# 64 bytes between the rings of split weights and their neighbours, and one slot instead of six for two small vectors

## The reference

```python
mod = (c_act @ w_ada + b_ada).reshape(B, N_MOD, 1, D_MODEL)
x = x + 0.5 * mod[:, 2] * swiglu(modulate(rmsnorm(x, norm_w[0]), mod[:, 0], mod[:, 1]), ffn1_wi, ffn1_wo)
h = modulate(rmsnorm(x, norm_w[1]), mod[:, 3], mod[:, 4])
zq, zk, zv, zb, zc, zu, zga, zgb = jnp.split(h @ w_in, splits, axis=-1)
o_attn = windowed_attention_with_context(q, k, v, kc, vc, sink)
y_conv = zb * short_conv(zc * zu, conv_w)
x = x + mod[:, 5] * gated_merge(o_attn, y_conv, zga, zgb, w_oa, w_ob, w_out)
x = x + 0.5 * mod[:, 8] * swiglu(modulate(rmsnorm(x, norm_w[2]), mod[:, 6], mod[:, 7]), ffn2_wi, ffn2_wo)
```

## Time and profile before

| | |
|---|---|
| time, median of 2 runs | 1981.53 us (1979.94 and 1983.12) |
| span of the profiled execution | 1978.3 us |
| granted clock of TensorE, mean over the span | 0.998 of full speed |
| TensorE busy | 1944.9 us, 98% of the span |
| VectorE busy | 867.2 us, 44% |
| ScalarE busy | 695.4 us, 35% |
| DMA engines, mean rate | 137 GB/s |

### The profile page before, as it was taken

One profiled execution on the slowest core, in us unless ns is written; L12 is line 12 of the kernel. 1 busy time (PEld: TensorE's weight loads), 2 busy tenths in 40 slices (PEclk: granted clock), 3 DMA queues, 4 the chain that ended last, 5 costly groups with the idle time before them and its releaser, 6 DMA issues.

```text
span 1978.3 us, 27290 instructions
## 1 busy us (share of the span) xinstructions
PE 1944.9 (98%) x10403; PEld 1587.5 (80%) x10403; DVE 867.2 (44%) x1337; ACT 695.4 (35%) x1050; POOL 92.1 (5%) x153
## 2 busy tenths in 40 slices
PE   6999999999999999999999999999999999999998
PEld 4666688887888888666668888888888889999998
DVE  4422333236665355433333226333322487666554
ACT  2422233124434324322233115333321355545543
POOL 1011100000000001111110000000000000000000
PEclk9999999999999999999999999999999999999999
DMA  8667622232222223666753222332332244446552
GB/s 300 221 220 250 234 86 97 94 85 81 74 70 64 75 94 119 233 234 224 240 192 97 96 90 80 96 95 95 96 96 95 64 129 128 141 137 191 181 190 97
DMA packets 183071, 271.17 MB, mean 137 GB/s; under 512 B 25196, under 2 KB 146268, under 8 KB 183004
## 3 DMA queue, kind: packets, MB, share of 16 engines
q1 hardware_dynamic: 164572, 203.12, 32.6%
q0 software_dynamic: 18432, 67.12, 10.1%
HBM read 269.16 MB, written 1.05 MB: 137 GB/s over the span
## 4 chain that ended last, share of the span: by engine, by line
PE 94%; DVE 4%; DMA 1%; ACT 0%; issue 0%; POOL 0%; SPq 0%; DVEq 0%; ACTq 0%
PE ps L440 29%; PE ps L442 28%; PE ps L441 28%; PE ps L464 4%; DVE T L1086 1%; DVE hL L1093 1%; PE ps L540 1%; PE ps L681 1%; PE ps L554 1%; PE ps L499 1%; DVE wL L1016 1%; PE ps L476 1%; DMA xin<-in_ctx 0%; PE ps L493 0%; PE ps L495 0%
## 5 line engine op out<-in xcount | busy, mean ns | idle before, releaser
L1016 DVE TENSOR_TENSOR wL<-raw,wH 128x1024 fp32r<-128x1024 f32 x364 | 442.4, 1224 | 668.5 <-ACT wH L804 666.9
L440 PE MATMUL ps<-hH,wH 128*128 128x512 f32 (+1 forms) x1984 | 714.8, 360 | 1.2 <-DVE hL L1348 0.9
L442 PE MATMUL ps<-hH,wL 128*128 128x512 f32 (+1 forms) x1984 | 703.6, 355 | 0.0
L441 PE MATMUL ps<-hL,wH 128*128 128x512 f32 (+1 forms) x1984 | 702.2, 354 | 0.0
L804 ACT ACTIVATE wH<-raw 128x1024 fp32r<-128x1024 f32 x364 | 383.1, 1058 | 685.0 <-PE ps L442 680.4
L440 PEld LDWEIGHTS ps<-hH,wH 128*128 128x128 f32 x1984 | 374.9, 189 | 97.6 <-issue 45.7
L442 PEld LDWEIGHTS ps<-hH,wL 128*128 128x128 f32 x1984 | 374.9, 189 | 53.9
L441 PEld LDWEIGHTS ps<-hL,wH 128*128 128x128 f32 x1984 | 375.3, 189 | 50.0
L440 PE MATMUL ps<-GH,wH 128*128 (+2 forms) x704 | 256.6, 365 | 0.0
L441 PE MATMUL ps<-GL,wH 128*128 (+2 forms) x704 | 256.6, 365 | 0.0
L442 PE MATMUL ps<-GH,wL 128*128 (+2 forms) x704 | 256.6, 365 | 0.0
(11 more groups left out here) (138 smaller groups left out, 1393.3 us busy)
## 6 DMA issues: line engine op xcount, KB each, us to landing
raw<-in_ffn_wi SPq DMA_DIRECT2D x176, 512.0 KB, 3.6
raw<-in_ffn_wo SPq DMA_DIRECT2D x88, 512.0 KB, 3.5
adaA<-in_w_ada POOLq DMA_DIRECT2D x64, 512.0 KB, 4.7
adaB<-in_w_ada POOLq DMA_DIRECT2D x64, 512.0 KB, 4.7
raw<-in_w_in SPq DMA_DIRECT2D x60, 512.0 KB, 3.9
raw<-in_w_out SPq DMA_DIRECT2D x16, 512.0 KB, 3.6
ada0b<-in_w_ada SPq DMA_DIRECT2D x4, 1024.0 KB, 13.6
raw<-in_w_in SPq DMA_DIRECT2D x32, 128.0 KB, 2.7
```

The lines of the kernel that those rows point to most:

```text
L440: mm(dst, wa, ra, start=start, stop=False, **kw)
L441: mm(dst, wa, rb, start=False, stop=False, **kw)
L442: return mm(dst, wb, ra, start=False, stop=stop, **kw)
L1016: tt(wL[:, s, :], raw[:, s, :], wH[:, s, :].bitcast(F32), ALU.subtract).then_inc(lo_done, 1)
```

## The change

Two arrays of 16 floats (64 bytes a partition) that nothing reads or writes are placed ahead of `wH` and behind `wL`. `normA` and `gateH` shrink from six slots to one, that is by 320 bytes each, and each norm and each residual now overwrites the slot of the one before. No instruction is added or removed and no wait is changed.

```diff
         raw = sb("raw", [P, RING, PIECE])
+        sb("beside_wH", [P, 16])
         wH = sb("wH", [P, RING, PIECE], F32R)
         wL = sb("wL", [P, RING, PIECE], F32R)
+        sb("beside_wL", [P, 16])
...
-        normA = sb("normA", [P, 3 * DEPTH, DC, 2])
-        gateH = sb("gateH", [P, 3 * DEPTH, DC, 2])
+        normA = sb("normA", [P, DC, 2])
+        gateH = sb("gateH", [P, DC, 2])
...
-                mark(stt(normA[:, v, ks], mod[:, mi + 1, ks], 1.0,
+                mark(stt(normA[:, ks], mod[:, mi + 1, ks], 1.0,
...
-                        stt(T[:, m % 2, cs], X[:, m, cs], normA[:, v, m, hf:hf + 1], ps[4][:, cs],
+                        stt(T[:, m % 2, cs], X[:, m, cs], normA[:, m, hf:hf + 1], ps[4][:, cs],
...
-                mark(ts(gateH[:, r - 1], mod[:, mi], 0.5, None, ALU.mult))
+                mark(ts(gateH[:], mod[:, mi], 0.5, None, ALU.mult))
...
-                        stt(X[:, m, cs], ps[bank_of(m)][:, cs], gateH[:, r - 1, m, hf:hf + 1], X[:, m, cs],
+                        stt(X[:, m, cs], ps[bank_of(m)][:, cs], gateH[:, m, hf:hf + 1], X[:, m, cs],
```

## The result

The changed kernel takes 2001.69 us (2001.33 and 2002.05), the kernel before 1981.53: a ratio of 1.0101, 95% interval 1.0085 to 1.0118. It is slower by 20.2 us. The profiled execution has a span of 1999.6 us, against 1978.3. In every execution on record the time is 1.6 to 1.8 us above its span, so the profile of the kernel before belongs to its faster run, 1979.94 us. The work of each engine has not changed (lines of the changed kernel are 2 higher than before, so L440 is L442 and L1016 is L1018).

A forecast was written before the change was run, and what follows sets the result against it. The prediction took TensorE's matmul start-to-start distances to bound the kernel; its terms, 28.2 - 8.7 - 10.6 - 1.3 + 3.9 = +11.5 us on 1981.5, gave 1993 us, with a range of 1980 to 2003 us.

The forecast's parts named there:

- exchange of the two relations: Main mechanism: hH takes GH's remainder 64 modulo 128 and GH takes hH's 0, so their matmul distances swap; 1988 to 1998 us.
- the one with the wider period: Rival: addresses count modulo 256 or more, so hH slows and GH stays slow; 1996 to 2006 us, chance 0.15.
- term 1: hH, hL matmuls at 512 columns: 4224 of them go from 226.7 to 233.3 ns, +28.2 us.
- What bounds the kernel: Whole kernel: TensorE, busy 98% of the span, so time is a count of matmuls by start-to-start distance.
- terms 3 and 4: GH, GL (-10.6 us) and QH, QL, YH, YL (-1.3 us) at 512 columns: each matmul 6.7 ns faster.
- term 5: At 256 columns GH, GL slow by 6.7 ns a matmul, +3.5 us, and QH and YH by 2.0, +0.4 us.
- term 2: hH, hL matmuls at 256 columns get faster: bounds -13.4 and -4.0 us, middle -8.7 taken.
- The costs taken as nothing: ScalarE's and VectorE's copies into the rings and the reused slots of normA and gateH: 0 us.
- a sign that it is wrong: TensorE's timeline: the prediction is wrong if stretches after an interruption follow another rule than steady ones; no size given.
- no effect of addresses: Rival: addresses don't matter to TensorE's matmul distances, so the time stays at 1981.5 us; chance 0.16.
- The other side: Rival: order matters and data 64 bytes behind the weights is good, so hH at 512 speeds up; 1945 us, chance 0.10.

The follow-up runs named there:

- both at zero: Kernel before with one slot each for norm scale and gate, no pads, 448 unused bytes ahead of adaA; hH and GH at remainder 0: 1974.62 us, 0.9963.

## Why the prediction came out as it did

The forecast was 1993 us, the range 1980 to 2003, the time 2001.7. Sign and range held, the main mechanism did not: no exchange of the two relations took place. The rival that holds is the one with the wider period, GH no faster than now, given 0.15, 1996 to 2006 us and 2001 at its middle. That the time lies inside the range was partly luck, since two misses of opposite sign met: with term 1 at the 28.2 us of the forecast and all else as measured it would have been near 2008.

**What bounds the kernel** was right: over all runs the distances of TensorE account for the difference in span from the kernel before to within 0.4 to 3.7 us, and 6.6 in the profiled execution of the run with only the slots; the norms with a clock at half are in this rest. The copies of ScalarE and VectorE kept their durations. **That the distance is a matter of the relation** between data and weights was right, and the run with everything shifted shows it apart from place. The forecast set rules of the Trainium skill beside it, and the runs show a difference that neither has. "SBUF — State Buffer", section "Who interferes with whom", has independent read ports; "TensorE: Matmul & The Clock Gate", section "Back-to-back issue gap", has columns / 2.4 + 2.5 ns, and gives this for a matmul by itself. The same matmuls at the same 2.4 GHz took 226.7 to 234.3 ns at 512 columns by address alone. Whether the two read ports hinder each other no run shows.

**The step that failed** is that the distance in bytes was taken modulo 128. The runs show 256: 0 and 128 differ by 5.7 to 6.6 ns at 512 columns, and 64 and 192 by 4.4. With 128 I read GH's new place, 128 modulo 256, as hH's old one, and so GH at 512 columns was to go to 226.7 ns and went to 232.4. I had two values of the relation in the rows, 0 and 192, and chose the smallest period that tells them apart; nothing in the rows preferred it to 256 or 512. Nor do distances lie on steps of 6.7 ns, as the forecast read them: 228.9, 231.1, 232.4 and 234.3 are means of patterns.

Term by term, by the sums over the trace:

1. hH at 512 columns: +28.2 forecast, +22.1 measured. The distance was right (233.3); the base was not 226.7 everywhere. Where thin matmuls, attention or a norm interrupt, the mean before was 227.4 to 228.6, which leaves less to lose; after the change the same stretches are at 233.3. Counting steady distances over 4224 matmuls made the forecast 28% larger than what was measured.
2. hH at 256: -8.7 forecast from bounds of -13.4 and -4.0, -5.6 measured. In the changed kernel its long SwiGLU input stage ran in the slower of the two patterns (117.8); with only the pads, where it ran in the faster one, it gave -9.5. The same relation has two patterns, and which one a stage falls into is not foreseen by anything I found.
3. GH, QH and YH at 512 (terms 3 and 4): -11.9 forecast, -1.7 measured. This is the failed step, and the bulk of the miss. Where GH was really at 0, in the run with both at zero, the two terms came to -11.8.
4. GH, QH and YH at 256 (term 5): +3.9 forecast, +2.8 measured, at 118.6 ns, not 120.

In sum +17.6 against +11.5: 10.2 too little for terms 3 and 4 and 3.1 for term 2, less 6.1 too much for term 1 and 1.1 for term 5. The other 2.6 us of the miss of 8.7 lie outside these terms; the norms with a clock at half, which change from execution to execution, are of this size. **The costs taken as nothing** were right: the slots alone made the kernel no slower, and the copies into the rings took 1058 and 1223 ns.

For term 1, a stretch of the kernel before behind thin matmuls: from the second matmul on 9 steps take 2.09 us, 232 ns each, and the next 13 take 2.94 us, 226:

```profile
105.32 0.39 PE L441 MATMUL ps<-hL,wH 128*128 128x512 f32 x1
...
107.41 0.39 PE L441 MATMUL ps<-hL,wH 128*128 128x512 f32 x1
...
110.35 0.39 PE L442 MATMUL ps<-hH,wL 128*128 128x512 f32 x1
```

The forecast named this as a sign that it is wrong, stretches after an interruption that follow another rule than the steady ones. The sign came true, and hH before the change is where it did.

The other rivals: no effect of addresses is refuted by nearly every run. The other side needed hH at 192 modulo 256 to differ from GH at 192; it took the same 233.3 at 512 columns.

## What to carry to other kernels

Where TensorE is the bound and weights are reloaded for every matmul, read the distance from start to start in each stage; equal matmuls at unequal distances may differ by where their data lies against their weights, and here the right place was worth 0.3% (one array moved) to 0.9% (most stages at their best remainder). Try the remainders of (data - weights) one by one, for each width of matmul that the kernel has: here 0 modulo 256 was best at 512 columns and 192 at 256 columns, and at 512 columns the neighbours of the best, 32 bytes off, were nearly as bad as any. Any change of the size of a small array moves all arrays behind it, so compare such relations before a small edit is blamed or praised for its instructions.

## What the runs showed of the hardware that was not expected

- The distance of fp32r matmuls that each load their own 128 by 128 weights goes by (data - weights) modulo 256 bytes (the period shown at 0, 128 and 192): 226.7 to 234.3 ns at 512 columns, 113.3 to 120.0 at 256, and not monotonically.
- 32 bytes off the best relation cost as much as 192 (233.3 ns).
- What is best at 512 columns (0) is, with 96, the worst at 256 (120.0).
- One relation can have two patterns: at 192, 256 columns ran at 113.3 or 117.8 ns, and at 512 columns as 233 throughout or as 231 and 236 in turn, with the same mean.
- ScalarE's and VectorE's copies hardly depend on the same offsets (1058 to 1061 and 1223 to 1224 ns).
- At which of the norms TensorE's clock falls to half differs between executions with the same distances: at the sixth in the kernel before (0.72 from 1770 to 1776 us), at the fifth with all arrays shifted (0.73 from 1574 to 1578 us).
